# A mixture-of-experts step on one Trainium2 core: gate and up as one 512-column product, and the slot work moved behind the put-back

## The reference

```python
for gi in range(N_GROUPS):
    sl = slice(gi * EXPERTS_PER_GROUP, (gi + 1) * EXPERTS_PER_GROUP)
    hg = jnp.einsum('td,edf->tef', x, w_gate[sl])
    hu = jnp.einsum('td,edf->tef', x, w_up[sl])
    hw = jax.nn.silu(hg) * hu * combine[:, sl, None]
    routed = routed + jnp.einsum('tef,efd->td', hw, w_down[sl])
```

## Time and profile before

| | us |
|---|---|
| launch, median of 3 runs | 1553.9 (1553.81 to 1555.06) |
| profiled execution, its span | 1551.6 |
| one turn of the expert loop, 616.33 to 632.20 | 15.87 |
| TensorE busy in the span | 1472.9 (95%) |
| VectorE busy in the span | 626.2 (40%) |
| ScalarE busy in the span | 299.1 (19%) |

### The profile page before, as it was taken

How to read it: one execution, slowest core, us unless ns; L and a number is a source line. 1 busy time by engine, 2 the same in 40 slices (tenths; PEclk the granted TensorE clock), 3 DMA queues, 4 the chain that set the end, 5 groups by cost and what they waited for, 6 DMA issues and landing times. The chain is left out here.

```text
span 1551.6 us, 29339 instructions
## 1 busy us (share of the span) xinstructions
PE 1472.9 (95%) x11071; PEld 982.9 (63%) x11071; DVE 626.2 (40%) x1628; ACT 299.1 (19%) x624; POOL 116.3 (7%) x122
## 2 busy tenths in 40 slices
PE   5999889989999999999998999799999999999996
PEld 2767777556666666666665688666666666666664
DVE  2038573723334343433335233733433334343434
ACT  0013112311111111111113221321111111111112
POOL 0000143000000000000000000100000000000000
PEclk8999798999999999999999999899999999999998
DMA  9996524779999999999993871389999999999971
GB/s 390 362 366 272 178 55 182 285 299 404 409 420 420 410 417 412 412 415 410 418 401 144 329 296 44 120 338 400 419 415 418 419 411 413 417 414 417 413 294 29
DMA packets 81361, 523.24 MB, mean 337 GB/s; under 512 B 14213, under 2 KB 14341, under 8 KB 21019
## 3 DMA queue, kind: packets, MB, share of 16 engines
q1 hardware_dynamic: 68587, 495.84, 78.6%
q0 software_dynamic: 12720, 26.63, 5.1%
HBM read 537.18 MB, written 4.74 MB: 349 GB/s over the span
## 5 line engine op out<-in xcount | busy, mean ns | idle before, releaser
L693 PE MATMUL psum<-ring,arena 128*64 128x256 f32 (+2 forms) x5552 | 706.7, 412 | 4.3 <-ACT arena L1264 2.3
L693 PEld LDWEIGHTS psum<-ring,arena 128*64 128x64 f32 (+1 forms) x5552 | 369.8, 139 | 297.8 <-issue 160.9
L1264 ACT ACTIVATE arena<-psum 128x256 f32<-128x256 f32 (+4 forms) x464 | 210.4, 489 | 1024.2 <-PE psum L693 529.0
L693 PE MATMUL psum<-arena 128*128 128x264 f32 (+2 forms) x1840 | 285.5, 324 | 4.1 <-DVE arena L1720 2.1
L693 PEld LDWEIGHTS psum<-arena 128*128 128x128 f32 (+1 forms) x1840 | 225.1, 171 | 62.7 <-issue 28.4
L1887 DVE TENSOR_TENSOR arena<-arena,psum 128x264 f32<-128x264 f32 x528 | 226.6, 429 | 9.3 <-PE psum L693 2.0
L693 PE MATMUL psum<-hT,ring 128*128 128x264 f32 x928 | 215.8, 390 | 6.2 <-DVE hT L1587 2.7
L693 PEld LDWEIGHTS psum<-hT,ring 128*128 128x128 f32 x928 | 176.4, 192 | 48.3 <-issue 19.9
L1914 DVE COPY arena<-psum 128x512 f32<-128x512 f32 x64 | 44.3, 692 | 274.1 <-PE psum L693 274.1
L654 POOL DMA_INDIRECT arena<-h_rows,slot_idx x68 | 67.6, 995 | 972.7 <-DVE slot_idx L1876 916.6
L696 PE MATMUL psum<-K,arena 128*128 128x128 f32 (+4 forms) x961 | 125.6, 270 | 7.3 <-DMA arena<-h_rows,slot_idx 5.4
(11 more groups left out here) (210 smaller groups left out, 478.8 us busy)
## 6 DMA issues: line engine op xcount, KB each, us to landing
ring<-in_moe_w_gate SPq DMA_DIRECT2D x128, 1024.0 KB, 11.4
ring<-in_moe_w_up SPq DMA_DIRECT2D x128, 1024.0 KB, 12.6
ring<-in_moe_w_down SPq DMA_DIRECT2D x128, 1024.0 KB, 9.5
ring<-in_w_mod SPq DMA_DIRECT2D x48, 1024.0 KB, 9.0
ring<-in_ab_w_in SPq DMA_DIRECT2D x13, 1024.0 KB, 7.8
ring<-in_gm_w_in SPq DMA_DIRECT2D x8, 1024.0 KB, 8.6
ring<-in_ab_w_out SPq DMA_DIRECT2D x4, 1024.0 KB, 5.7
ring<-in_gm_w_out SPq DMA_DIRECT2D x4, 1024.0 KB, 6.9
```

The source lines that it names most:

```text
L693: return nc.tensor.matmul(out, lhsT, rhs, start=start, stop=stop)
L1264: return nc.scalar.activation(out, in_, func, **kw)
```

## The change: one product for gate and up, a new place for the slot work

The two products become one: each matmul takes the gate and the up columns of an expert together, 512 columns, and writes a whole bank (bank 0: gate in its first half, up in its second). There are 16 matmuls in place of 32. All four units must have arrived and stay in use until the product ends, so the ring holds gate and up of one expert next to each other and `unit_used` counts four steps a turn in place of six. The transposes of `ghid` go to bank 1, which is free now.

The selector's transposes, `slots()`, move on TensorE from between the two products to behind the put-back. On VectorE `take_slots` moves from ahead of the multiplication to behind the eight additions. ScalarE's order stays.

```diff
-RU = NPAIR * PU
+UNIT_OF = ((0, 0), (0, 1), (1, 0), (1, 1), (0, 2), (1, 2))
+USED_AT = (1, 1, 2, 2, 3, 4)
+USES = 4
+RU = NPAIR * USES
...
-                sp.dma_start(ring[:, eslot(j), :], expert_src(l, pair2 + (j // PU * 2 + j % 2), j % PU // 2)).then_inc(eload[eslot(j)], 16)
+                sp.dma_start(ring[:, eslot(j), :], expert_src(l, pair2 + (j // PU * 2 + UNIT_OF[j % PU][0]), UNIT_OF[j % PU][1])).then_inc(eload[eslot(j)], 16)
...
-                            def product(kind):
-                                arrived_units(kind)
-                                for c in range(DT):
-                                    for e in range(2):
-                                        x = mm(psum[64 * e:64 * e + 64, kind, 0:DE], xgT[:, c, 64 * e:64 * e + 64],
-                                               ring[:, s0 + 2 * kind + e, c * DE:(c + 1) * DE], c == 0, c == DT - 1)
-                                        if c == DT - 1:
-                                            x.then_inc(S["unit_used"], 1)
...
-                            product(0)
-
-                            pe.wait_ge(S["sel"], r * SEL_R + i * EBODY + (b + 3))
-                            slots()
-
-                            pe.wait_ge(S["ghid"], done1 - 1 + ONE)
-                            product(1)
+                                    if c == 0:
+                                        arrived_unit(2 * e)
+                                        arrived_unit(2 * e + 1)
+                                    x = mm(psum[64 * e:64 * e + 64, 0, :].rearrange("p (k f) -> p k f", k=2), xgT[:, c, 64 * e:64 * e + 64],
+                                           ring[:, s0 + 2 * e:s0 + 2 * e + 2, c * DE:(c + 1) * DE], c == 0, c == DT - 1)
+                                    if c == DT - 1:
+                                        x.then_inc(S["unit_used"], 1)
...
                                 mm(psum[:, back_bank(c), 0:T], gout_tiles[:, c], selT[(b + 3) % 4]).then_inc(S["cb_mm"], 1)
 
+                            pe.wait_ge(S["sel"], r * SEL_R + i * EBODY + (b + 3))
+                            slots()
+
                             pe.wait_ge(S["ghid"], done1 + ONE)
                             for j in range(2):
-                                last = tr(psum[:, 0, (2 + j) * P:(3 + j) * P], ghid[:, j])
+                                last = tr(psum[:, 1, j * P:(j + 1) * P], ghid[:, j])
                             last.then_inc(S["ht_mm"], 1)
...
                             take_weights(b, i * 8 + 2 * b, r * XT_R + i * 8 + (2 * b + 2))
-                            take_slots((b + 2) % 4, r * SEL_R + i * EBODY + (b + 3))
-
                             dve.wait_ge(S["gsil"], done1 + ONE)
                             dve.wait_ge(S["wt_set"], done1 + ONE)
-                            dve.wait_ge(S["unit_used"], used0 + 4 + ONE)
+                            dve.wait_ge(S["unit_used"], used0 + 2 + ONE)
...
                             add_back(r * CB_R + i * 32 + 8 * b)
-                            dve.wait_ge(S["unit_used"], used0 + 6 + ONE)
+                            take_slots((b + 2) % 4, r * SEL_R + i * EBODY + (b + 3))
+                            dve.wait_ge(S["unit_used"], used0 + 4 + ONE)
```

More of the change, by code:

```diff
@@ L528, in experts @@
                 with sp.Fori(first, end) as r:
-                    with sp.Fori(0, RU // ESLOTS - 1) as i:
+                    with sp.Fori(0, NPAIR * PU // ESLOTS - 1) as i:
                         for j in range(ESLOTS):
-                            sp.wait_ge(S["unit_used"], r * RU + i * ESLOTS + (j + 1) + ONE)
+                            sp.wait_ge(S["unit_used"], r * RU + i * (2 * USES) + (j // PU * USES + USED_AT[j % PU]) + ONE)
                             expert_load(l, (i + 1) * 4, j)
@@ L535, in experts @@
                         for j in range(ESLOTS):
-                            sp.wait_ge(S["unit_used"], r * RU + (RU - ESLOTS) + (j + 1) + ONE)
+                            sp.wait_ge(S["unit_used"], r * RU + (RU - 2 * USES) + (j // PU * USES + USED_AT[j % PU]) + ONE)
                             expert_load(l, 0, j)
@@ L1108, in moe, with arrived_unit @@
                             s0 = eslot((b % 2) * PU)
-                            def arrived_units(kind):
-                                for e in range(2):
-                                    pe.wait_ge(eload[s0 + 2 * kind + e], r * (RU // ESLOTS * 16) + i * 32 + 16 * (b // 2 + 1))
-                            def product(kind):
-                                arrived_units(kind)
-                                for c in range(DT):
-                                    for e in range(2):
-                                        x = mm(psum[64 * e:64 * e + 64, kind, 0:DE], xgT[:, c, 64 * e:64 * e + 64],
-                                               ring[:, s0 + 2 * kind + e, c * DE:(c + 1) * DE], c == 0, c == DT - 1)
-                                        if c == DT - 1:
-                                            x.then_inc(S["unit_used"], 1)
-                            pe.wait_ge(S["xt_sb"], r * XT_R + i * 8 + (2 * b + 2))
-                            pe.wait_ge(S["gsil"], done1 - 1 + ONE)
-                            product(0)
-                            pe.wait_ge(S["sel"], r * SEL_R + i * EBODY + (b + 3))
-                            slots()
-                            pe.wait_ge(S["ghid"], done1 - 1 + ONE)
-                            product(1)
+                            def arrived_unit(u):
+                                pe.wait_ge(eload[s0 + u], r * (NPAIR * PU // ESLOTS * 16) + i * 32 + 16 * (b // 2 + 1))
+                            pe.wait_ge(S["xt_sb"], r * XT_R + i * 8 + (2 * b + 2))
+                            pe.wait_ge(S["ghid"], done1 - 1 + ONE)
+                            for c in range(DT):
+                                for e in range(2):
+                                    if c == 0:
[5 more added lines that the diff above has]
+                                        x.then_inc(S["unit_used"], 1)
                             pe.wait_ge(S["os_a"], done1 - 1 + ONE)
@@ L1148, in moe @@
                             pe.wait_ge(S["ht_sb"], done1 + ONE)
-                            arrived_units(2)
+                            arrived_unit(4)
+                            arrived_unit(5)
                             for n in range(2):
@@ L1415, in moe @@
                             done1 = r * NPAIR + i * EBODY + (b + 1)
-                            used0 = r * RU + i * (EBODY * PU) + b * PU
+                            used0 = r * RU + i * (EBODY * USES) + b * USES
                             act.wait_ge(S["unit_used"], used0 + 2 + ONE)
@@ L1422, in moe @@
                             act.wait_ge(S["ht_mm"], done1)
+                            act.wait_ge(S["unit_used"], used0 + 2 + ONE)
+                            f(ghT, psum[:, 1, 0:2 * P].rearrange("p (j s) -> p j s", j=2), ACT.Copy).then_inc(S["ht_sb"], 1)
+                            rows_in(r * XT_R + i * 8 + (2 * b + 2))
                             act.wait_ge(S["unit_used"], used0 + 4 + ONE)
-                            f(ghT, psum[:, 0, 2 * P:4 * P].rearrange("p (j s) -> p j s", j=2), ACT.Copy).then_inc(S["ht_sb"], 1)
-                            rows_in(r * XT_R + i * 8 + (2 * b + 2))
-                            act.wait_ge(S["unit_used"], used0 + 6 + ONE)
                             f(gout_tiles[:, :, 0:64], psum[:, 2, :].rearrange("p (d c) -> p c d", c=DT), ACT.Copy).then_inc(S["os_a"], 1)
@@ L1901, in moe @@
                             done1 = r * NPAIR + i * EBODY + (b + 1)
-                            used0 = r * RU + i * (EBODY * PU) + b * PU
+                            used0 = r * RU + i * (EBODY * USES) + b * USES
                             choose(i * 8 + (2 * b + 4))
                             take_weights(b, i * 8 + 2 * b, r * XT_R + i * 8 + (2 * b + 2))
-                            take_slots((b + 2) % 4, r * SEL_R + i * EBODY + (b + 3))
                             dve.wait_ge(S["gsil"], done1 + ONE)
                             dve.wait_ge(S["wt_set"], done1 + ONE)
-                            dve.wait_ge(S["unit_used"], used0 + 4 + ONE)
-                            V.scalar_tensor_tensor(ghid.rearrange("p j f -> p f j"), gsil.rearrange("p (f j) -> p f j", j=2), wt[:, b:b + 1], psum[:, 1, 0:DE].rearrange("p (f j) -> p f j", j=2), ALU.mult, ALU.mult).then_inc(S["ghid"], 1)
+                            dve.wait_ge(S["unit_used"], used0 + 2 + ONE)
+                            V.scalar_tensor_tensor(ghid.rearrange("p j f -> p f j"), gsil.rearrange("p (f j) -> p f j", j=2), wt[:, b:b + 1], psum[:, 0, DE:2 * DE].rearrange("p (f j) -> p f j", j=2), ALU.mult, ALU.mult).then_inc(S["ghid"], 1)
                             dve.wait_ge(S["cb_add"], r * CB_R + i * 32 + 8 * b + BACK0)
                             add_back(r * CB_R + i * 32 + 8 * b)
-                            dve.wait_ge(S["unit_used"], used0 + 6 + ONE)
```

(2 more changed lines are left out.)

## The result

The changed kernel takes 1591.45 us (median of 4 runs, 1590.23 to 1593.28), the one before 1554.48 beside it: ratio 1.024, 95% interval 1.0222 to 1.0257. It is slower by 37 us; 39 were forecast. The ends of the interval stand for 34.5 and 40.0 us. The profiled execution, the longest of the four runs, spans 1591.1 us against 1551.6, 39.5 more, and as before its TensorE is on the full granted clock in the loop.

The account below looks back on a forecast made before the run. TensorE's own stream was taken to bound the loop at 15.87 us a turn; -0.56 + 0.23 + 0.47 + 0.47 = +0.61 us, times 64 turns is +39 us, giving 1593 us, range 1574 to 1612 (80%).

Parts of the forecast that it names:

- gate, selector, up become one product: TensorE's stretch at the turn's start shrinks from 7.54 to 6.98 us: 0.56 saved a turn, bounds 0.54 to 0.58.
- selector behind the put-back: The selector's three transposes, now after the put-back on TensorE, add 0.23 us a turn, up to 0.27.
- wait at the put-back's fourth tile: TensorE waits for the late first addition to free its bank: +0.47 us a turn, bounds 0.39 to 0.55.
- wait ahead of the next tokens: Before rows_in, TensorE waits for ScalarE to copy the selector from bank 4: +0.47 us a turn, bounds 0.42 to 0.57.
- The total: All terms together lengthen a turn by 0.61 us, to 16.48 from 15.87; over 64 turns, 39 us.
- first wait: In the put-back, the fourth tile waits for the first addition, delayed by Silu and multiplication: +0.47 us a turn.
- second wait: Between the selector's transposes and the next tokens, TensorE waits for ScalarE's copy: +0.47 us a turn.
- The bound: In the expert loop TensorE's own stream sets the turn, 15.87 us; its only stops are at changes of tile shape.
- The product: Joined gate and up product takes 6.98 us, 0.4286 a wide slot; gate, selector and up shrink by 0.56 a turn.
- little of it is width: Most of the product's 0.56 us saving is one fewer crossing into the selector and back, plus the selector's own 0.23.
- What moves at nothing: Later take_slots, gather (six us of cover) and release of gate units (3.9 us later) cost TensorE nothing.
- The rival of a falling clock: TensorE's granted clock falls to 0.50 around the selector, doubling some 1.4 us a turn: 1683 us; chance 4%.

Follow-up runs that it names:

- four_banks: The changed kernel with four banks in turn for the put-back instead of three, selector still behind the put-back; 1567.0 us, ratio 1.0096 to the kernel before.
- selector_ahead: The changed kernel with the selector's transposes moved to between the wide product and the put-back; 1543.7 us, ratio 0.9942 to the kernel before.
- narrow_selector_ahead: The kernel before, two 256-column products kept, selector's transposes moved between up product and put-back, take_slots behind the additions; 1533.4 us, ratio 0.9872.
- ahead_and_four_banks: The changed kernel with the selector between wide product and put-back and also four put-back banks; 1535.4 us, ratio 0.9877 to the kernel before.
- tokens_ahead: The changed kernel with the selector between wide product and put-back, and take_slots back ahead of the multiplication on VectorE; 1602.8 us, ratio 1.0306.

## Why the prediction was right, step by step

| term, us a turn | forecast | measured |
|---|---|---|
| gate, selector, up become one product | -0.56 | -0.58 (7.54 to 6.96) |
| selector behind the put-back | +0.23 | +0.23 (not seen apart from its wait) |
| wait at the put-back's fourth tile | +0.47 | +0.38 |
| wait ahead of the next tokens | +0.47 | +0.55 (0.51, and 0.04 in the transposes behind it) |
| first turn of an iteration, spread over four | none | +0.04 |
| sum | +0.61 | +0.62 |

- **The total** is nearer than its terms. The first wait was forecast too long by 0.09, the second too short by 0.08, the product's gain too small by 0.02, and 0.04 was missed; that these cancel to 0.01 is luck. The first wait, 0.38, lies just outside its bounds of 0.39 to 0.55; the product and the second wait are inside theirs. That both waits are there, where forecast, and that each goes when its own cause is taken away, is not luck: four_banks takes the first and leaves the second, selector_ahead takes the second and most of the first.
- **The bound** was right: TensorE's stream and its waits add up to the turn in the kernels whose pieces are read here. The reading of the earlier trace rows was too simple: 251 stops in some 25 turns are ten a turn, and eight of them are the 0.29 behind a pair of the down product, not changes of tile shape. As these are inside the pace of 0.43, the sum does not change.
- **The product**: right, and that "little of it is width" is shown: narrow products without the selector between them save the same but for 0.04 us. What is saved is a crossing between tile shapes: taking the selector from between the narrow products to behind them (narrow_selector_ahead; `take_slots` moves too, which by itself changes nothing) shortens the turn by 15.87 - 15.56 = 0.31. The wide slot was 0.43, as forecast. The Trainium skill has a rule for the crossing on "TensorEngine Tiling (Array Packing)", section "Key Properties": a change of the tiling mode drains TensorE. The trace agrees as far as leaving a product costs some 0.12 by the prediction's sum; no row shows a drain as such. The Trainium skill also gives the share of weight loads, beside the share of the peak arithmetic reached, as a measure of TensorE's headroom ("Perfetto Trace Analysis", section "Identifying the Most-Contended Engine"). That halving the loads should gain time is the prediction's own step and not on that page, and it did not hold: the share of PEld fell from 63% to 53% and the kernel became slower, and the two fastest kernels, 2 us apart, have it at 64% (narrow_selector_ahead) and 56% (ahead_and_four_banks).
- **The first wait** was there, mis-sized by 0.09. The handoffs were right (0.12 for an assumed 0.11), but the first addition starts 0.51 behind the multiplication and not 0.61: the 0.61 of the earlier trace rows held the put-back's own first tile, which had not ended sooner. In narrow_selector_ahead, where the multiplication stands ahead of the put-back, the addition comes 0.83 behind it:

```profile
604.03 0.67 DVE L1908 SCALAR_TENSOR_TENSOR arena<-arena,psum 128x256 f32<-128x256 f32 x1 [5.53 <-PE psum L693]
...
604.86 3.54 DVE L1887 TENSOR_TENSOR arena<-arena,psum 128x264 f32<-128x264 f32 x8
```

  The removal of the wait by a fourth bank shows that the bank is its cause.
- **The second wait** was 0.55 and not 0.47. ScalarE starts 0.43 behind the selector's first transpose, as forecast, and ends at about 0.82; the rest is the way back to TensorE, 0.10 or so instead of 0.05, and the first transposes behind it. It goes where the selector stands ahead of the put-back.
- **The first turn of an iteration** was missed. Before, Silu is late there too: its starts are 15.94 and then 15.80 us apart around such a turn, the second row here, while every turn is 15.87. The delay was covered.

```profile
445.53 0.66 ACT L1264 ACTIVATE arena<-psum 128x256 f32<-128x256 f32 x2 [2.94 <-PE psum L693]
...
461.47 0.67 ACT L1264 ACTIVATE arena<-psum 128x256 f32<-128x256 f32 x2 [3.00 <-PE psum L693]
...
477.27 0.67 ACT L1264 ACTIVATE arena<-psum 128x256 f32<-128x256 f32 x2 [2.94 <-PE psum L693]
```

  After, ScalarE and VectorE are 0.07 and 0.10 later there, and TensorE waits for both. The register steps of the loop are the likely cause: they precede both instructions. It is argued only; no kernel with another unrolling was run.
- **What moves at nothing**: shown for `take_slots` by itself, and for the gather with it, in the kernel before. The gate units come free 3.4 us later (6.98 against 3.55 into the turn), not 3.9. In the changed kernel, whose turns are long, TensorE does not wait for the ring; where the turn is down to 15.52, late units cost some 3.4 us a launch (read row by row in one of the ten long turns). Whether that is their late release or the early need of the up units was not taken apart.
- The rival of a falling clock fell: 1.00 in the window above.

## What to carry to other kernels

When two products that share an input are joined, look for what ran under the second one: here Silu and a multiplication had their cover there, and a step that is moved to the end of the chain loses its cover as well. Before moving work on the bounding engine, write down which two of its instructions a chain through the other engines will then lie between, and add up the chain from neighbouring rows; the same saving was to be had, with neither wait, by leaving the products narrow and putting the three transposes between the second product and the put-back (with `take_slots` behind the additions; whether that part is needed there was not run). And when an engine that hides a transfer becomes faster, follow the landing times over the whole loop, not in one turn: the lead can be spent slowly.

## What was not expected of the hardware

- The DMA's rate was a floor that no wait showed. In the kernel before, the loads came at a share of 1.01 and TensorE never waited; with a turn of 15.56 us the landing time of an up unit grows over a layer from 13.7 to 20.8 us, and TensorE still does not wait. It does in ahead_and_four_banks, with a turn of 15.52 and a form that needs its up units 3.4 us earlier.
- The chain from the product through ScalarE and VectorE is longer in the first turn of an iteration, by 0.17 us. It costs as much as is not covered: 0.17 in the changed kernel and selector_ahead, 0.24 in tokens_ahead, 0.10 in four_banks, nothing in ahead_and_four_banks or in the narrow kernels. The distance of two multiplications on VectorE shows it even where TensorE does not wait, so the turn has to be read on the engine that bounds the loop.
